# Transposing the residual rows of a transformer block: scaled by 1/rms on VectorE first, or multiplied by a diagonal on TensorE

## What is computed

```python
x = x + 0.5 * swiglu_ffn(rms_norm(x, ffn1_norm[l]), ffn1_w_gu[l], ffn1_w_down[l])
h = rms_norm(x, mix_norm[l])          # feeds three branches, merged and added to x
x = x + merged @ w_out[l]
x = x + memory_cross_attention(rms_norm(x, xattn_norm[l]), rms_norm(mem, mem_norm[l]), ...)
x = x + 0.5 * swiglu_ffn(rms_norm(x, ffn2_norm[l]), ffn2_w_gu[l], ffn2_w_down[l])
```

## Time and profile before

| | us |
|---|---|
| median of 3 runs | 1606.1 |
| lowest, highest | 1605.19, 1607.34 |
| span of the profiled execution | 1607.0 |

### The profile page before, as it was taken

One profiled execution on the slowest core, in us unless ns is written; L12 is line 12 of the kernel. 1 busy time (PEld: TensorE's weight loads), 2 busy tenths in 40 slices (PEclk: granted clock), 3 DMA queues, 4 the chain that ended last, 5 costly groups with the idle time before them and its releaser, 6 DMA issues.

```text
span 1607.0 us, 28515 instructions
## 1 busy us (share of the span) xinstructions
PE 1485.1 (92%) x10469; PEld 1382.9 (86%) x10469; DVE 874.8 (54%) x1325; ACT 737.5 (46%) x1220; POOL 52.3 (3%) x118
## 2 busy tenths in 40 slices
PE   6599989989989988999989999898999998799997
PEld 5599979878989777999989999887898998699996
DVE  4355554678665644555455555467776464455553
ACT  4244444744544444444454444455455444354442
POOL 2000000000000100000000000000000001000000
PEclk9799999989999999999999999999999999999999
DMA  7766655343434532656646666453343354256661
GB/s 171 212 182 183 196 160 158 106 132 106 157 105 158 184 105 80 184 181 183 189 147 190 183 183 205 127 157 106 109 154 105 126 189 132 79 150 190 183 183 66
DMA packets 286298, 244.85 MB, mean 152 GB/s; under 512 B 14216, under 2 KB 263464, under 8 KB 286208
## 3 DMA queue, kind: packets, MB, share of 16 engines
q1 hardware_dynamic: 283856, 236.77, 48.6%
q0 software_dynamic: 1040, 2.63, 1.1%
q10 hardware_dynamic: 1312, 4.25, 0.8%
HBM read 240.99 MB, written 2.64 MB: 152 GB/s over the span
## 4 chain that ended last, share of the span: by engine, by line
issue 96%; POOLq 2%; POOL 1%; DVE 0%
POOLq L628 1%; POOL diag L629 1%; POOLq L623 1%; POOLq L625 0%; POOL rstd L626 0%; DVE final_out L1256 0%; POOL brow_dram L636 0%; POOL fb L597 0%; POOLq L618 0%; POOLq L606 0%; POOL wx L605 0%; POOL wa L604 0%; POOLq L614 0%; POOL causal L600 0%; POOL chunked L601 0%
## 5 line engine op out<-in xcount | busy, mean ns | idle before, releaser
L455 DVE TENSOR_TENSOR w_lo<-raw,w_hi 128x1024 fp32r<-128x1024 f32 x444 | 528.8, 1220 | 290.1 <-ACT w_hi L447 289.7
L447 ACT ACTIVATE w_hi<-raw 128x1024 fp32r<-128x1024 f32 x444 | 447.8, 1050 | 158.2 <-PE acc L1331 121.8
L1369 PE MATMUL work<-act_hi,w_hi 128*128 128x256 f32 x1408 | 399.7, 284 | 17.1 <-DVE w_lo L455 13.9
L1369 PE MATMUL work<-act_lo,w_hi 128*128 128x256 f32 x1408 | 399.1, 283 | 0.0
L1369 PE MATMUL work<-act_hi,w_lo 128*128 128x256 f32 x1408 | 399.1, 283 | 0.0
L1369 PEld LDWEIGHTS work<-act_hi,w_hi 128*128 128x128 f32 x1408 | 268.8, 191 | 19.5 <-DVE w_lo L455 14.1
L1369 PEld LDWEIGHTS work<-act_hi,w_lo 128*128 128x128 f32 x1408 | 268.8, 191 | 1.8
L1369 PEld LDWEIGHTS work<-act_lo,w_hi 128*128 128x128 f32 x1408 | 268.8, 191 | 0.0
L1294 PE MATMUL work<-act_hi,w_hi 128*128 128x256 f32 x848 | 250.0, 295 | 14.3 <-DVE act_lo L937 8.9
L1294 PE MATMUL work<-act_hi,w_lo 128*128 128x256 f32 x848 | 245.4, 289 | 0.0
L1294 PE MATMUL work<-act_lo,w_hi 128*128 128x256 f32 x848 | 245.2, 289 | 0.0
(11 more groups left out here) (216 smaller groups left out, 1808.6 us busy)
## 6 DMA issues: line engine op xcount, KB each, us to landing
raw<-in_ffn_w_gu SPq DMA_DIRECT2D x176, 512.0 KB, 4.9
raw<-in_w_in SPq DMA_DIRECT2D x52, 1024.0 KB, 5.2
raw<-in_ffn_w_down SPq DMA_DIRECT2D x44, 1024.0 KB, 4.9
raw<-in_w_branch SPq DMA_DIRECT2D x12, 1024.0 KB, 5.0
raw<-in_w_mkv SPq DMA_DIRECT2D x8, 1024.0 KB, 5.0
raw<-in_w_out SPq DMA_DIRECT2D x8, 1024.0 KB, 4.9
raw<-in_w_mq SPq DMA_DIRECT2D x4, 1024.0 KB, 5.8
raw<-in_w_mo SPq DMA_DIRECT2D x4, 1024.0 KB, 5.0
```

The costliest lines, as they stand in the source:

```text
L447: eng.activation(halves(w_hi, slot, kind, part), halves(raw, slot, kind, part), ACT.Copy)\
L455: eng.tensor_tensor(halves(w_lo, slot, kind, part), halves(raw, slot, kind, part), halves(w_hi, slot, kind, part).bitcast(F32), ALU.subtra ...
L1369: mm = pe.matmul(work[:, c, g * SEQ:g * SEQ + SEQ], ww[:, c, at_w:at_w + P], xx[:, k, :], start=(k == 0 and q == 0 and g == 0), stop=(k == ...
```

## The change

VectorE scales both row tiles of x by 1/rms into a new buffer `xs` (over `merged`) right after the residual, or at the layer's start ahead of the first splits, and TensorE transposes from `xs` with the identity in transpose mode. GpSimd makes no diagonal any more; for mem it scales the rows of `mem_x` in place. SP's wait ahead of the load of `final_gain`, which shares `merged`, is now for the last transposes.

```diff
+        xs = at("xs", [P, TT, D], over="merged")
-        diag = at("diag", [P, TT, P])
+        xs_ready = sem("xs_ready")
@@ SP, at the end
-            sp.wait_ge(x_ready, 4 + 16 * (DEPTH - 1) + 12)
+            sp.wait_ge(job_done, (DEPTH - 1) * JOBS + PLAN.jobs[("nt", 3, 3)] + 1)
@@ GpSimd
-            def power(l, n, tt, diagonal=True):
+            def power(l, n, tt, over_rms=None):
...
-                if diagonal:
+                if over_rms is not None:
                     g.drain()
-                    e = g.tensor_scalar(diag[:, tt, :], ident[:], rstd[:, tt:tt + 1], None, ALU.mult)
+                    e = g.tensor_scalar(over_rms[:, tt, :], over_rms[:, tt, :], rstd[:, tt:tt + 1], None, ALU.mult)
                 e.then_inc(rstd_ready, 1)
...
-                        power(l, n, tt, n != 2)
+                        power(l, n, tt, mem_x if n == 3 else None)
@@ VectorE
+            def over_rms(l, n):
+                place = (0, 1, 4, 5)[n]
+                for tt in range(TT):
+                    v.wait_ge(rstd_ready, l * 12 + (2 * place + tt + 1))
+                    v.tensor_scalar(xs[:, tt, :], x[:, tt, :], rstd[:, tt:tt + 1], None, ALU.mult).then_inc(xs_ready, 1)
...
                 v.drain().then_inc(gain_ready, 1)
+                over_rms(l, 0)
                 for part in range(2):
                     split_lo(v, l, (0, 0, 0), part)
...
                 residual(l, 0, 0.5)
+                over_rms(l, 1)
                 norm_los(l, 1, 1)
...
                 residual(l, 1, 1.0)
+                over_rms(l, 2)
                 splits(v, split_lo, l, "out3")
...
                 residual(l, 2, 1.0)
+                over_rms(l, 3)
                 norm_los(l, 3, 4)
@@ TensorE
-            def rows_over_rms(l, name, k, tt, src):
-                return pe.matmul(ps2(name)[:, k % 2, tt * P:tt * P + P], src[:, tt, k * P:(k + 1) * P], diag[:, tt, :],
-                                 start=True, stop=True)
+            def transpose_rows(l, name, k, tt, src):
+                return pe.transpose(ps2(name)[:, k % 2, tt * P:tt * P + P], src[:, tt, k * P:(k + 1) * P], ident[:])
@@ in transposes, and likewise for mem_x
-                    pe.wait_ge(rstd_ready, l * 12 + (2 * place + tt + 1))
+                    pe.wait_ge(xs_ready, l * 8 + (2 * n + tt + 1))
```

More of the change, by code:

```diff
@@ L1265, in ready @@
                 pe.wait_ge(lo_ready, l * (2 * UNITS) + u0 * 2 + (part + 1 + 2 * RING))
-            def rows_over_rms(l, name, k, tt, src):
-                return pe.matmul(ps2(name)[:, k % 2, tt * P:tt * P + P], src[:, tt, k * P:(k + 1) * P], diag[:, tt, :],
-                                 start=True, stop=True)
+            def transpose_rows(l, name, k, tt, src):
+                return pe.transpose(ps2(name)[:, k % 2, tt * P:tt * P + P], src[:, tt, k * P:(k + 1) * P], ident[:])
             def transposes(l, n):
-                place = (0, 1, 4, 5)[n]
                 for j in range(4):
@@ L1277, in transposes @@
                 for tt in range(TT):
-                    pe.wait_ge(rstd_ready, l * 12 + (2 * place + tt + 1))
+                    pe.wait_ge(xs_ready, l * 8 + (2 * n + tt + 1))
                     for k in range(KT):
-                        mm = rows_over_rms(l, ("nt", n, k // 2), k, tt, x)
+                        mm = transpose_rows(l, ("nt", n, k // 2), k, tt, xs)
                         if tt == TT - 1 and k % 2:
@@ L1522, in _ @@
                             for tt in range(TT):
-                                mm = rows_over_rms(l, ("mt", s - 13), k, tt, mem_x)
+                                mm = transpose_rows(l, ("mt", s - 13), k, tt, mem_x)
                         mm.then_inc(job_done, 1)
```

## The result

| | runs | median us | lowest, highest | mean granted clock of the runs |
|---|---|---|---|---|
| before | 6 | 1606.5 | 1605.2, 1608.2 | 0.968 (17 later runs) |
| changed | 6 | 1613.3 | 1609.3, 1617.5 | 0.960 |

What follows compares the result with a forecast made beforehand. TensorE, busy 92% of the span, was taken as the bound, then waits, the longest at the start. Terms +5.6 +6.9 +1.3 +1.2 -1.0 -0.6 -0.9 -1.05 gave +11.4 us, 1617.5 as a median; range 1608.5 to 1623.

Steps and rivals of the forecast that it cites:

- Start: First layer's start: slot 0's load falls behind the bias table's DMA, so pair 2 starts later, +5.6 us (+5 to +8.5).
- Granted clock: Norms 1 and 3, layer 2's norm 0: fewer TensorE records lower the clock, +6.9 us (0 to 12).
- Second layer's start: Layer 2's norm 0: VectorE's two scalings come ahead of its first splits and make norm_lo late, +1.3 us.
- Inside norms 1 and 3: TensorE saves two records on the path at each of these norms, -0.24 us each, -1.0 in all.
- norm 2: Scaling and first split are covered by mk1's TensorE work; a saving of -0.3 us, twice, -0.6 in all.
- mem's rows: Memory rows' transposes: one of four record groups a layer keeps its saving, -0.47 us a layer, -0.9 in all.
- end: Last norm: without the diagonal the last final_out starts earlier, -1.05 us.
- GpSimd's scaling of mem_x: Memory stage: two scalings a layer, 3.6 us each, may make VectorE wait for the port; +0.6 a layer, +1.2.
- 1 (the load gets through): Start: slot 0's second half lands before 30 us; 1602.9 us (chance 0.07), or 1609.8 with the clock term (0.08).
- 2 (the clock holds): Norms: TensorE's bursts stay regular and the clock holds, start as forecast; 1610.6 us, chance 0.2.
- 3: Memory stage: GpSimd's scaling takes 5.3 us and shuts VectorE out, about 3 us a layer; 1622.3 us, chance 0.08.
- 4: TensorE's transposes: transposing costs two records as well, so TensorE's and clock terms go; 1612.5 us, chance 0.02.

Runs made afterwards that it cites:

- e8: Changed kernel, with GpSimd issuing the bias table's DMA only after the sixth act_hi, behind both halves of slot 0's load: 1608.1 us.
- e5: Kernel before, with the bias table row written 16 times instead of 128 and fetched by eight loads: 1587.9 us.
- e6: Changed kernel, with the bias table row written 16 times instead of 128 and fetched by eight loads: 1583.8 us.
- e1: Changed kernel, with VectorE at norm 0 writing slot 0's two w_lo halves before it scales the row tiles: 1615.8 us.
- e10: e6 with added transposes of the identity, results unused, where TensorE would stand still in the norms: 1582.6 us.
- e3: Changed kernel, with the scaled rows turned by an ordinary fp32 product with the identity instead of the transposing mode: 1613.3 us.
- e2: Changed kernel, with GpSimd issuing the bias table's DMA ahead of norm 0's two power chains: 1617.9 us.
- e4: Changed kernel, with every transpose of the norms' and mem's rows issued twice into the same place: 1613.7 us.

## Why the prediction was right, and where its size was not

**Start, +5.6 forecast.** The mechanism is shown (e8, e5, e6). The chain came out as written: scaling 0.75 us each, slot 0's load behind the table, split at 51.18 (forecast 52.9), TensorE idle from 30 to 53.88 (forecast 31 to 55.5), the second wait of pair 1 gone. Measured: +3.5 at pair 2, below the lower end of +5. The 2.1 us too much are spread over the chain: the table was issued at 14.07 and not at 15.2 (0.83 us of that is an earlier setup in this execution, 0.3 is GpSimd's chain), the split followed the table's end by 2.7 us and not by 3.2, and pair 2 followed TensorE's restart by 24.3 us and not by 24.8. And the cause was placed wrongly in part. The prediction put it on VectorE's order first; e1 shows that the missing diagonal alone is enough.

**Granted clock, +6.9.** Place and direction are right: half clock at norms 1 and 3 in both layers and at layer 2's norm 0, nowhere there before, and e10 shows the cause. At norms 1 and 3 the products behind the norm cost 1.0 + 1.4 + 1.6 + 1.6 = 5.6 us (forecast 2 x 1.7 + 2 x 0.9 = 5.2). What the forecast left unsaid is that the half-clock stretches elsewhere would stay as they were. They did not. In this pair of profiles they gave back some 7 us (0.5 = 3.5 start + 0.7 inside the norms + 5.6 - 1.2 end - 1.0 for mem's rows, less 7.1). Norm 2 has 3.4 us at half clock where it had 6.8.

**Second layer's start, +1.3, and 1.7 of the clock term.** Residual to first product grew by 1.8 us, clock included (forecast 3.0). What was overlooked: with the diagonal, tile 0's products ran beside VectorE's turn of the loop; now both scalings come behind it, TensorE stands 4.4 us, and the clock falls over the transposes. TensorE there in the kernel before:

```profile
817.18 2.05 PE L1269 MATMUL work<-diag,x 128*128 128x128 f32 x16 [0.98 <-POOL diag L629]
819.92 2.05 PE L1269 MATMUL work<-diag,x 128*128 128x128 f32 x16 [0.69 <-POOL diag L629]
```

**Small terms.** Inside norms 1 and 3 -0.01 to -0.19 (forecast -0.25 each), norm 2 -0.37 each (forecast -0.3), mem's rows -0.5 a layer (forecast -0.47), end -1.2 (forecast -1.05). GpSimd's scaling of mem_x took 3.4 us in the mean (forecast 3.6): 2.87 for the first of a layer and 3.97 for the second, which runs beside VectorE's work. VectorE was held by it once a layer, one of the signs that the prediction had named as speaking against it, but no TensorE wait came of it, so +1.2 should have been 0:

```profile
431.21 1.21 DVE L456 TENSOR_TENSOR w_lo<-raw,w_hi 128x1024 fp32r<-128x1024 f32 x1
...
432.57 1.11 DVE L1188 TENSOR_TENSOR lg<-lg,ri 128x256 f32<-128x256 f32 x1
```

The multiply, 0.42 us in the earlier trace rows, takes 1.11 beside a scaling that runs from 431.19 to 435.16.

**The total.** By the terms that could be placed in the two traces, the change was forecast 4.6 us too large for these reasons: the start by 2.1, VectorE's wait for GpSimd by 1.2, clock and second start together by 0.8 (8.2 forecast, 7.4 measured), the small terms by 0.3, and what came back elsewhere by 0.8; against that, 0.6 less was won inside norms 1 and 3. The placed terms add up to 7.6 us, and the medians differ by 6.8 (interval 4.7 to 9.2). The 7 us given back in the pair of profiles are no measure for the medians: 6.3 of them are where the two profiled executions lie against their medians. The sign is not luck: the start, the clock at the norms and layer 2's start all point that way. The nearness is in part luck, since the forecast had no term for what the clock does in the attention. The forecast's own range also took 4 us either way for the clock, where the term's own ends, 0 and 12, lie 6.9 below and 5.1 above.

**Rivals.** 1 (the load gets through) is refuted by the wait of 26.6 us. 2 (the clock holds) is refuted at norms 1 and 3 and at layer 2's norm 0, though its value, 1610.6, is nearer to the median (2.7 us) than the forecast's (4.2). 3 is refuted in its price, not in its mechanism. 4: the trace has 128 records for 256.

**What stays open.** The clock outside the start does not repeat between kernels as the stages would have it. The changed kernel's six runs have clocks from 0.957 to 0.962 and spread over 8 us along with them, while the four of e6, with the same norms, all have 0.970 and spread over 2 us. Behind the start, the changed kernel's median loses about 3 us (6.8 - 3.5) to the kernel before, while e6 gains about 3 (4.1 - 1.2) on e5. And where the clock is held behind norm 1, it falls in the attention some 100 us later (26 cases of 28). What ties the two places together was not found.

## What to carry to other kernels

Before you price a change of work, look up which DMA it lets start sooner: a long transfer that is issued 3 us earlier, ahead of a weight load and not behind it, cost more here than all the work removed was worth, and making that transfer small was worth 18 to 29 us. Where TensorE stands still in short gaps, work taken off it there comes back as a lower clock; price the gap, not the busy time. And a clock that is held in one place can be lost in another: e3 and e10 won 5.9 and 9.5 us at the norms and lost 5.0 and 7.8 in the attention, so look over the whole span. When a change moves the clock, compare several runs with their granted clocks: one pair of profiles showed 0.5 us here and the medians 6.8.

## What the runs showed of the hardware

- In e2 GpSimd's next step behind a `drain` came 33.8 us late, 0.2 us after a DMA that GpSimd itself had issued had landed; in e1 the like gap is 0.16 us.
- Transposes of 128x128 fp32 in the transposing mode, two sets or with fillers, went with a granted clock of 1.00 where one set alone had 0.74 (e4, e10).
- A half-clock stretch that was kept away behind norm 1 came back some 100 us later in the stream: windows on the same products show 0.83 in e3 and e10 where the changed kernel and e6 have 1.00.
- GpSimd's 128x1024 scaling went with a VectorE multiply of two inputs that took 1.11 us instead of 0.42, but ended 1.5 us before the scaling did; the w_lo ahead of it and the one behind it kept their 1.2 us. The Trainium skill, "SBUF — State Buffer", section Who interferes with whom, has a VectorE instruction with two SBUF inputs contend with a GpSimd one that reads SBUF, and says of VectorE's two-port modes that whoever comes first has the pair for the whole instruction; the row agrees with the first and does not show the whole length.
- Writing 1.5 MB from 8 partitions took 34.4 us and 0.19 MB took 6.2 us. Behind the first ScalarE waited 26.6 us for a weight load; behind the second no product of the start waited for one.
